# The embedding gate of a four-block kernel: both passes by rows, eight units each, with its first four weight units in homes of their own

## The reference

```python
gate, up = jnp.split(rms_norm_2(h, g_ffn_pre) @ w_ffn_in, 2, axis=-1)
h = h + rms_norm_2((jax.nn.silu(gate) * up) @ w_ffn_out, g_ffn_post)
e = p_i @ w_ple_proj
h = h + rms_norm_2(jax.nn.sigmoid(h @ w_ple_gate) * e, g_ple_post)
return h
```

## Time and profile before

| | us |
|---|---|
| median of three runs | 1835.9 |
| lowest and highest | 1835.85, 1836.21 |
| the profiled execution's own time | 1835.64 |
| its span, first to last instruction | 1833.8 |
| TensorE matmuls busy | 1816.5 |
| VectorE busy | 1197.2 |
| ScalarE busy | 983.3 |
| GpSimd busy | 127.9 |

### The profile page before, as it was taken

How to read it: one execution, slowest core, us unless ns; L and a number is a source line. 1 busy time by engine, 2 the same in 40 slices (tenths; PEclk the granted TensorE clock), 3 DMA queues, 4 the chain that set the end, 5 groups by cost and what they waited for, 6 DMA issues and landing times.

```text
span 1833.8 us, 24654 instructions
## 1 busy us (share of the span) xinstructions
PE 1816.5 (99%) x8930; PEld 1502.5 (82%) x8930; DVE 1197.2 (65%) x2064; ACT 983.3 (54%) x1565; POOL 127.9 (7%) x52
## 2 busy tenths in 40 slices
PE   8999999999999999999999999999999999999998
PEld 7887888888888888888877888888877788888886
DVE  6766873556776874455767867555677686675556
ACT  5556554444555654445655656544557366464444
POOL 0000018300000008500000000000000000000000
PEclk9999999999999999999999999999999999999999
DMA  7544555556544655555644445656556354555563
GB/s 248 154 140 136 195 193 175 184 191 194 169 144 138 198 167 188 180 186 178 197 144 142 147 161 172 206 158 211 173 169 194 104 167 139 175 178 187 174 211 109
DMA packets 167771, 315.31 MB, mean 172 GB/s; under 512 B 10250, under 2 KB 22748, under 8 KB 167524
## 3 DMA queue, kind: packets, MB, share of 16 engines
q1 hardware_dynamic: 167332, 313.14, 53.6%
q10 hardware_dynamic: 320, 0.60, 0.1%
HBM read 312.65 MB, written 1.05 MB: 171 GB/s over the span
## 4 chain that ended last, share of the span: by engine, by line
PE 95%; DVE 3%; issue 1%; ACT 1%; DMA 0%; ACTq 0%; DVEq 0%
PE acc L598 84%; PE mix L565 4%; PE mix L850 1%; PE mix L657 1%; PE mix L645 1%; PE mix L863 1%; DVE lo L1576 1%; PE mix L891 1%; PE mix L904 1%; PE mix L625 1%; PE mix L825 0%; PE mix L922 0%; PE mix L839 0%; PE mix L859 0%; PE mix L830 0%
## 5 line engine op out<-in xcount | busy, mean ns | idle before, releaser
L1109 ACT ACTIVATE hi<-raw 128x1024 fp32r<-128x1024 f32 (+3 forms) x596 | 612.0, 1032 | 518.5 <-PE acc L598 487.5
L1576 DVE TENSOR_TENSOR lo<-raw,hi 128x1024 fp32r<-128x1024 f32 (+3 forms) x548 | 641.7, 1186 | 232.5 <-ACT hi L1109 218.0
L598 PE MATMUL acc<-hi,xTh 128*128 128x512 f32 (+3 forms) x1712 | 669.5, 391 | 1.3 <-DVE xTl L1615 1.3
L598 PE MATMUL acc<-hi,xTl 128*128 128x512 f32 (+3 forms) x1712 | 653.9, 382 | 0.0
L598 PE MATMUL acc<-lo,xTh 128*128 128x512 f32 (+3 forms) x1712 | 652.9, 381 | 0.0
L598 PEld LDWEIGHTS acc<-hi,xTh 128*128 128x128 f32 x1712 | 322.4, 188 | 69.9 <-issue 9.4
L598 PEld LDWEIGHTS acc<-hi,xTl 128*128 128x128 f32 x1712 | 322.2, 188 | 62.3
L598 PEld LDWEIGHTS acc<-lo,xTh 128*128 128x128 f32 x1712 | 322.7, 188 | 57.8 <-issue 1.0
L1077 POOL TENSOR_TENSOR lo<-raw,hi 128x1024 fp32r<-128x1024 f32 x48 | 127.6, 2688 | 634.7 <-ACT hi L1109 634.7
L598 PE MATMUL acc<-hi,hTh 128*128 128x512 f32 x432 | 169.0, 391 | 0.0
L598 PE MATMUL acc<-hi,hTl 128*128 128x512 f32 x432 | 168.2, 389 | 0.0
(11 more groups left out here) (255 smaller groups left out, 1671.1 us busy)
## 6 DMA issues: line engine op xcount, KB each, us to landing
raw<-in_w_in SPq DMA_DIRECT2D x192, 512.0 KB, 3.5
raw<-in_w_ffn_in SPq DMA_DIRECT2D x80, 512.0 KB, 4.4
raw<-in_w_mlp_up SPq DMA_DIRECT2D x64, 512.0 KB, 3.6
raw<-in_w_mlp_down SPq DMA_DIRECT2D x64, 512.0 KB, 4.4
raw<-in_w_ffn_out SPq DMA_DIRECT2D x44, 512.0 KB, 4.5
raw<-in_w_out SPq DMA_DIRECT2D x32, 512.0 KB, 4.3
raw<-in_w_o_gla SPq DMA_DIRECT2D x16, 512.0 KB, 3.7
raw<-in_w_o_attn SPq DMA_DIRECT2D x16, 512.0 KB, 3.8
```

What stands on the lines that cost most here:

```text
L598: last = nc.tensor.matmul(out, a[:, t * P:(t + 1) * P], w[:, part, :], start=(k == 0 and a is ah and w is hi), stop=(k == c.k_tiles - 1 an ...
L1109: nc.scalar.activation(L.plan.part(L.hi, u, L.hi_early), L.plan.part(L.raw, u), ACT.Copy).then_inc(*n.up("hi_ready"))
L1576: v.tensor_tensor(lo, raw, hi.bitcast(F32), ALU.subtract).then_inc(*n.up("low_by_dve"))
```

## The change

The gate is done for row 0 in units 152 to 159, with the eight transposes of row 1 after unit 155, and then for row 1 with its halves turned round: 156 to 159 first, then 152 to 155 (`turn`). The transposes for the gate put four k tiles in a bank, and ScalarE and VectorE split a bank in one instruction of 128x512. Units 152 to 155 of blocks 2 and 3 have homes for highs and lows outside the ring: two in the arena of the attention part, two in the tiles over the hidden rows, where the last block's first two units also lie; its third and fourth go into the ring. In block 2 the transposes of block 3's row 0 stand between the two halves of row 1. The opening of block 3 does four units for row 0 (three before) ahead of row 1's transposes. The orders on ScalarE and VectorE are written anew. The number of signals for banks falls by two each on banks 0 and 2.

```diff
@@ Plan
-        self.early = {self.base[-1] + i: i for i in range(RING)}
+        gates = [self.base[ln] + PLE_FIRST for ln in range(LAYERS, BLOCKS)]
+        self.early = {u + i: (i // 2, i % 2) for u in gates for i in range(RING)}
+        self.early.update({self.base[-1] + i: (1, 2 + i) for i in range(2)})
...
+    def turn(self, u):
+
+        i = u - self.base[self.unit[u][0].ln] - PLE_FIRST
+        return u - i + (i + RING) % (2 * RING) if self.unit[u][0].name == "ple" else u
...
     def before(self, u):
-        return u - 2 * RING if u - RING in self.early else u - RING
+        v = u - RING
+        while v in self.early:
+            v -= RING
+        return v
@@ tensor_program
     def unit(u):
-        products(u, (1,) if u in begun else (0, 1), (1,) if u in halved else (0, 1)).then_inc(*n.up("unit_used"))
+        v = L.plan.turn(u)
+        products(v, (1,) if v in begun else (0, 1)).then_inc(*n.up("unit_used"))
...
-        turn_rows("g", 0, x_tile)
+        turn_rows("g", 0, x_tile, (0,))
         s.to(152)
-        rest_of_rows("g", 152)
-        s.to(156)
+        pe.wait_ge(*n.next("x_rows"))
+        turn_rows("g", 0, x_tile, (1,))
+        first_rows(156)
+        pe.wait_ge(*n.next("x_rows", NT))
+        turn_rows("g", 1, x_tile)
         first_rows(160)
         if ln + 1 < BLOCKS:
-            s.to(159)
-            products(s.plan.base[ln] + 159, (1,), (0,))
+            s.to(156)
             ln += 1
             pe.wait_ge(*n.next("x_rows"))
             turn_rows("x", 0, x_tile)
             ln -= 1
-            halved.add(s.u)
         s.to(160)
...
-        first_rows(u + (3 if tag == "x" else 2))
-        pe.wait_ge(*n.next("x_rows"))
+        first_rows(u + (4 if tag == "x" else 2))
+        pe.wait_ge(*n.next("x_rows", 2 if tag == "x" else 1))
         turn_rows(tag, 1, x_tile)
@@ scalar_program, opening of block 3
+            squares_of_row(0)
             s.to(1)
             split_rows("x", 1, x_gain(ln))
-            squares(L.x, 0)
             s.to(2)
             split_half("x", 1, x_gain(ln))
-            squares(L.x, 1)
+            squares_of_row(1)
@@ scalar_program, the gate
         square_of(b, 0)
         root(VAR_X, POST, 1)
-        s.to(151)
-        split_rows("g", 0)
+        s.to(150)
+        split_rows("g", 0, banks=(0,))
         square_of(b, 1)
         root(VAR_X + 1, POST + 1, 1)
         s.to(152)
         embedded(L.plan.chunk(ln, "plain", COLS))
-        s.to(153)
+        split_rows("g", 0, banks=(1,))
+        s.to(157)
         split_rows("g", 1)
-        s.to(154)
-        split_half("g", 1)
...
-        s.to(157)
...
         if ln + 1 < BLOCKS:
             highs(opening + 3)
-        gated(a, 1)
-        if ln + 1 < BLOCKS:
-            highs(opening + 4)
-        s.to(159)
-        if ln + 1 < BLOCKS:
             ln += 1
             split_rows("x", 0, x_gain(ln))
             ln -= 1
-            gated(b, 1)
-            s.to(160)
-            gated_square(a, 1)
-        else:
-            gated(b, 1)
-            gated_square(a, 1)
+            highs(opening + 4)
+        gated(a, 1)
+        gated_square(a, 1)
+        gated(b, 1)
         gated_square(b, 1)
@@ vector_program, opening of block 3
-            s.to(1)
+            s.to(2)
             gated_with_gain(a, 1)
             dve.wait_ge(*n.next("squared", 2))
             mean_of_rows(1)
             inverse_root_of_rows(1)
             add_normed(1, 0)
-            s.to(2)
-            split_rows("x", 1, x_gain(ln))
-            gated_with_gain(b, 0)
             gated_with_gain(b, 1)
             tell("gain2_free")
-            add_normed(0, 1)
+            split_rows("x", 1, x_gain(ln))
             add_normed(1, 1)
@@ vector_program, the gate
         refine(0)
         add_normed(0, 0)
+        s.to(150)
+        add_normed(0, 1)
         s.to(151)
-        split_rows("g", 0)
+        split_rows("g", 0, banks=(0,))
         dve.wait_ge(*n.next("squared"))
         mean_of_rows(1, "variance")
         s.to(152)
         refine(1)
         add_normed(1, 0)
-        s.to(154)
         with_gain(b, 1, 1)
         tell(f"pair{b.pair}_drained")
         tell("gain1_free")
+        add_normed(1, 1)
+        split_rows("g", 0, banks=(1,))
+        s.to(158)
         split_rows("g", 1)
-        add_normed(0, 1)
-        add_normed(1, 1)
-        s.to(155)
-        split_half("g", 1)
         gain_landed(2)
...
-        s.to(158)
         gated(a, 0)
-        gated_with_gain(a, 0)
-        if ln + 1 < BLOCKS:
-            opening = L.plan.base[ln] + L.plan.size[ln]
-            lows(opening + 1)
-            gated(b, 0)
-        else:
-            gated(b, 0)
-            gated_with_gain(b, 0)
+        if ln + 1 == BLOCKS:
+            gated_with_gain(a, 0)
+        gated(b, 0)
+        gated_with_gain(*((a if ln + 1 < BLOCKS else b), 0))
...
         if ln + 1 < BLOCKS:
+            opening = L.plan.base[ln] + L.plan.size[ln]
             add_normed(0, 0)
             lows(opening + 2)
-            s.to(160)
-            sigmoid_read(a)
             ln += 1
             split_rows("x", 0, x_gain(ln))
             ln -= 1
+            s.to(160)
+            sigmoid_read(a)
             gated(a, 1)
+            gated_with_gain(b, 0)
+            add_normed(0, 1)
             sigmoid_read(b)
             gated(b, 1)
         else:
+            add_row(0)
             gated(a, 1)
             tell(f"pair{a.pair}_drained")
-            add_row(0)
```

More of the change, by code:

```diff
@@ L109 @@
 RING = 4
+PLE_FIRST = 152
 I32 = mybir.dt.int32
@@ L285, in by_rows, with used, ends_of @@
     def by_rows(self, c, j):
[L287 removed]
+        return c.ln >= LAYERS and (c.tag == "g" or j < 2 and (c.tag == "f" or c.tag == "x" and c.ln > LAYERS))
+    def turn(self, u):
+        i = u - self.base[self.unit[u][0].ln] - PLE_FIRST
+        return u - i + (i + RING) % (2 * RING) if self.unit[u][0].name == "ple" else u
+    def used(self, u):
+        return self.turn(u) + 1
+    def ends_of(self, c, t):
+        return (self.turn(c.first), self.turn(c.final)) if c.name == "ple" and t else (c.first, c.final)
     def part(self, ring, u, early=None):
         c = self.unit[u][0]
[L292 removed]
+        home, slot = self.early[u] if early is not None and u in self.early else (None, u % RING)
+        tiles = ring if home is None else early[home]
         return tiles[:, slot, 0:min(2, c.k_tiles), 0:c.n]
     def before(self, u):
[L297 removed]
+        v = u - RING
+        while v in self.early:
+            v -= RING
+        return v
     def chunk(self, ln, name, to):
@@ L574, in tensor_program, with products @@
     y_tile = lambda t, k: L.y[:, t, k * P:(k + 1) * P]
-    def products(u, rows, tiles=(0, 1)):
+    def products(u, rows):
         c, j = L.plan.unit[u]
         hi, lo = L.plan.part(L.hi, u, L.hi_early), L.plan.part(L.lo, u, L.lo_early)
-        if u == c.first and c.turn:
+        first, final = L.plan.ends_of(c, rows[-1])
+        if u == first and c.turn:
             if c.after_rows and rows == (0,):
@@ L591, in products @@
         pe.wait_ge(*n.at(*L.plan.low[u]))
-        for part in tiles[:c.k_tiles]:
+        for part in range(min(2, c.k_tiles)):
             k = 2 * j + part
@@ L614, in first_rows, with turn_rows @@
                 last.then_inc(*n.up("rows0_done"))
-    def turn_rows(tag, t, rows):
-        for j in range(2):
-            fill((tag, "rows", t, j), lambda b: [nc.tensor.transpose(L.mix[:, b, i * P:(i + 1) * P], rows(t, 2 * j + i), L.ident) for i in range(2)])
+    def turn_rows(tag, t, rows, banks=(0, 1)):
+        tiles = 4 if tag == "g" else 2
+        for j in banks:
+            fill((tag, "rows", t, j), lambda b: [nc.tensor.transpose(L.mix[:, b, i * P:(i + 1) * P], rows(t, tiles * j + i), L.ident) for i in range(tiles)])
     def scores(tag, h, q, k):
@@ L1104, in high @@
         if u in L.plan.early:
-            out = next(c for c in L.plan.chunks if c.ln == BLOCKS - 2 and c.weight == "w_ffn_out_2" and c.to == COLS)
-            act.wait_ge(*n.at("unit_used", out.final + 1))
+            out = [c for c in L.plan.chunks if c.weight == "w_ffn_out_2" and c.to == COLS and c.first < u][-1]
+            if L.plan.early[u][0]:
+                act.wait_ge(*n.at("unit_used", out.final + 1))
         elif u >= RING:
-            act.wait_ge(*n.at("unit_used", L.plan.before(u) + 1))
+            act.wait_ge(*n.at("unit_used", L.plan.used(L.plan.before(u))))
         nc.scalar.activation(L.plan.part(L.hi, u, L.hi_early), L.plan.part(L.raw, u), ACT.Copy).then_inc(*n.up("hi_ready"))
@@ L1197, in squares, with squares_of_row @@
             square(rows[:, t, g * COLS:(g + 1) * COLS], parts + 2 * g + t)
+    def squares_of_row(t):
+        for g in range(2):
+            act.wait_ge(*n.next("x_rows"))
+            square(L.x[:, t, g * COLS:(g + 1) * COLS], PARTS + 2 * g + t)
     def softmax_exp(tag, h, scale):
@@ L1622, in split_half, with split_rows @@
             split(tag, j, gain=gain)
```

(4 more changed lines are left out.)

34 lines of the change are left out of this document (17 added, 17 removed).

## The result

| | before | after |
|---|---|---|
| median, us (five runs each) | 1835.85 | 1843.69 |
| lowest and highest | 1834.02, 1836.21 | 1843.56, 1844.73 |
| the profiled execution's own time | 1835.64 | 1843.56 |
| its span | 1833.8 | 1841.7 |

After over before is 1.0048, with an interval of 1.0037 to 1.0059: 7.8 us slower. The spans of the two profiled executions differ by 7.9 us, so the two traces can be laid side by side and have to account for all of it. The five times before and after don't overlap.

What follows compares the result with a forecast made beforehand. TensorE's matmul stream, busy 99% of the span, was taken as the bound. Two gates of 5.2 us (10.4), opening +0.5 and end -0.3 gave +10.6 on 1835.64: 1846.2 us, range 1840 to 1850.5.

Steps and rivals of the forecast that it cites:

- VectorE's order holds low 154: Gate, VectorE: four things newly ahead of low 154 make it ready at 1322.7, where TensorE comes to it at 1319.2.
- Low 153 stands for its high: Gate: ScalarE makes high 153 behind row 1's root, so VectorE stands 1.46 us before low 153.
- The split of 128x512: Gate, VectorE: each wide split out of PSUM takes 0.70 us, bounded by 0.69 and 0.76.
- The stall, 3.5 in each gate: TensorE waits 3.5 us for low 154 before unit 154 in blocks 2 and 3; bounds 2.0 to 3.7.
- The late load, +0.7: Gate: unit 158's load waits for low 154; TensorE waits 0.4 there, some 0.3 at 159; bounds 0 to 2.0.
- The clock, +1.7 in each gate: Behind each gate's stall TensorE's clock falls as in the old opening, costing 1.7 us and swallowing the late load's 0.7.
- The forecast's words for a clock that stays at 1.00: Sign: if row-0 products break in the gate but the clock stays at 1.00, the time is 1843 to 1844.
- The opening, +0.5: Block 3's opening: waits of 2.8 become 2.8 to 3.8 at other places, with the same clock fall; 0.5 us more.
- The end, -0.3: Program's end: row 0 ends earlier, so the gated product starts at about 1826.5 instead of 1826.80; 0.3 us gained.
- the smaller stall: Rival, 14%: high 153 doesn't hold VectorE, 2.0 us per gate, and no clock fall behind it; +4.3, 1840.
- The worse loads: Rival, 10%: loads take 5.6 us to land, unit 158 waits some 2 us in each gate; +14.1, 1850.
- The faster one: Rival, 6%: homes bring highs and lows ahead of need, block 3's opening loses its gaps and clock fall; -4.8, 1831.

Runs made afterwards that it cites:

- Experiments 1: Kernel after, with VectorE's lows 154 and 155 moved ahead of y, the second add of x and the second split: 1838.02 us, ratio 1.0014.
- experiment 5: Kernel before, with VectorE's y for row 1's second half and both second-half adds of x put ahead of lows 154 and 155: 1838.93 us, ratio 1.0019.
- experiment 2: Kernel after, with ScalarE's high 153 made ahead of row 1's square and root: 1840.87 us, ratio 1.0025.
- experiment 6: Kernel after, with SyncE holding the load of block 3's first unit until high 159 of block 2 is ready: 1844.14 us, ratio 1.0047.
- Experiment 9: Kernel of 7, with ScalarE's high 155 ahead of its second split and VectorE's two signals behind its split: 1834.56 us, ratio 0.9995.
- experiment 3: Kernel after, with lows 154 and 155 moved ahead on VectorE and high 153 moved ahead on ScalarE: 1836.27 us, ratio 1.0005.
- experiment 4: Kernel before, with homes outside the ring for highs and lows of units 152 and 153 in both gates: 1835.77 us, ratio 0.9999.
- 7: Kernel of experiment 3, with lows of the opening's units 2 and 3 ahead of VectorE's sigmoid read: 1835.38 us, ratio 0.9999.
- 10: Kernel of Experiment 9, with three units instead of four for row 0 ahead of row 1's transposes in block 3's opening: 1834.65 us, ratio 0.9995.
- experiment 8: Kernel of 7, with low 156 of both gates made by GpSimd instead of VectorE: 1835.37 us, ratio 0.9999.

## Why the prediction was right

The forecast was 1846.2, in a range of 1840 to 1850.5, with 0.89 on slower; 1843.69 came out, slower by 0.43%. The way and the mechanism are right; the size is 2.5 us too large, and the term that was mis-sized most is the clock. By its own steps:

- **VectorE's order holds low 154.** Right, and the main step. Low 154 started at 1321.04 where 1321.35 was worked out. From the add of x(0, first half) to it the forecast had 11.3 us, the trace 10.8 (1310.23 to 1321.04). Experiments 1 and 5 show it from both sides: taken out of after, the wait shrinks from 2.76 to 0.44; put into before, one of 1.53 appears.
- **Low 153 stands for its high.** Right: 1.32 us for 1.46, and experiment 2 gave 1.3 back in each gate.
- **The split of 128x512.** It lasts 0.68, but the next instruction starts 0.60 behind it (1314.08 to 1314.68), and the forecast's chain adds such distances. So its 0.70 was 0.1 too much, twice, and its lower bound of 0.69 too high.
- **The stall, 3.5 in each gate.** The mechanism is right and the size 0.6 too large: 2.9, twice. The chain was 0.5 us shorter than forecast: 0.2 by the two splits, 0.1 by the stand for high 153, and the rest by the lows, which follow at 1.14 and not 1.18. TensorE came to unit 154 0.1 later (behind the transposes ahead of unit 152 the second product starts 0.32 us after the first, 1316.94 after 1316.62, and not 0.23).
- **The late load, +0.7.** Mis-sized, inside its bounds of 0 to 2.0, and it fell on another unit. Unit 158 was to be late by 0.4 and 159 by 0.3. The load of 158 landed in 3.6 us and wasn't late; that of 159 took 5.9, with two more issued behind it within some 2.3 us, and was late by 1.6 in block 2. In block 3, where no loads follow, it took 4.5. That is most of why there is no wait there: low 159 is done at 1820.01, 7.9 us behind the start of unit 154, and TensorE at full clock would want it after 7.8. The fall of the clock swallowed only the 0.2 that would have been left with the hand-over. The fit that the forecast took from the Trainium skill, "DMA: Bandwidth & Descriptors", section "Anatomy of one DMA — SWDGE (gpsimd) path", is for loads issued by GpSimd; its estimate of 3.2 us for 512 KB lies under all of these loads, which SyncE issued. The nearest to it is the 3.6 us of a load that started with no other in flight.
- **The clock, +1.7 in each gate.** This is the term that carries most of the error. The forecast took one fall before as a rule for every gap of its size and expected three. The profiled execution after had one, behind a wait of 2.77 us, and none behind the same wait 490 us earlier. Net of the opening, where the fall of before stayed away, the clock cost 0 where +3.4 was forecast. The forecast's words for a clock that stays at 1.00, 1843 to 1844, fit the number but not the trace: there was a fall in block 3, and one less in the opening. That they fit is partly luck. The three falls that were forecast did come in experiment 6, with the same waits at unit 154, and that execution took 1845.15.
- **The opening, +0.5.** Right that waits are exchanged: 3.1 us, at the places named, for a forecast of 2.8 to 3.8. Before has 3.0 when it is read by starts, so the difference is +0.1. "The same fall" was wrong, -1.7.
- **The end, -0.3.** Right: -0.25.

The forecast with the measured terms in place of its own: 3.4 less for the clock, 1.2 less for the two stalls, 1.6 more for the load (its sum held nothing for it, since the fall was to swallow it), 0.4 less in the opening's waits. 1846.2 - 3.4 - 1.2 + 1.6 - 0.4 = 1842.8, and the profiled execution took 1843.56. Of the 0.8 between them, 0.2 is the beginning and 0.2 the slow second products behind the new holes, neither of them in the forecast; 0.4 is rounding or isn't assigned. That the stall was too large (1.2) and the load too small (1.6) cancelled is luck. The weak step is the one from a single fall in the trace of before to a rule for every gap of its size.

Of the rivals, the smaller stall (1840) had one reason wrong, as high 153 did hold VectorE, and one half right: there was one example of a fall, and behind one of the two gaps none came. The worse loads (1850) had the right mechanism for block 2, but on unit 159 and not 158, 1.6 us for some 2, and once and not twice. The faster one, 1831, needed low 154 done by 1319.2. Experiment 9 shows that this can be had by order alone, and that the gain is then still not 4.8: waits of 0.4 and 1.2 us stay in the opening, and one of 0.4 in block 2's gate.

## What to carry to other kernels

Where orders are written out by hand, list for each engine what the new order puts ahead of the next thing that the busiest engine needs, and sum it against the slack; here the place of two lines cost 7.4 of the 7.8 us, the homes were free, the turned halves were worth 4 us once the orders were right, and with both lines in place the whole change lay within 0.4 us of before. A buffer that is free early helps only if the producers' orders reach the unit early, and each late low passes its delay on through the slot that it frees to the load four units on. Before a change is given up, look for the one or two lines of order that hold it: the same design with four lines of order added and two signals moved (experiment 9) lies 9 us lower.

## What the runs showed of the hardware that was not expected

**The clock doesn't fall behind every gap of one size.** In the profiled execution after, two waits of 2.76 and 2.77 us with the same instructions around them were followed by a clock of 1.00 and by 0.80, 0.50, 0.50, 0.50. In experiment 6 both such waits were followed by 0.50. The opening shows the same with smaller waits: behind 0.91 and 1.19 us, with four transposes between, the clock fell in the traces of experiments 1, 2 and 6 and not in those of after and experiment 3; behind 1.14 and 0.69 it fell in before and experiment 5 and not in experiment 4. Single waits of up to 1.53 us (experiments 2, 5, 7 to 10) had no fall behind them in any trace. The times of the kernel before agree with that: over its 84 runs in three batches those with a mean clock of 0.999 have a median of 1834.5 us, the others, two in three, 1836.2. A mean clock doesn't say where it fell, but the difference of 1.7 us is the 1.7 read from the earlier trace rows, so a fall there that comes and goes from run to run is the likely reason. What decides it is open. In experiments 9 and 10, where no wait but those at the program's start is longer than 1.5 us, all 22 runs are at 0.999.

**Loads close together.** In block 2's gate after, 512 KB landed in 3.6 us for the first of four loads, and in 5.9, 6.0 and 6.1 us for the three issued behind it, each some 1.1 us after the one before.

**VectorE beside GpSimd.** In experiment 8 an add of 128x512 took 1.98 us in place of 0.75 while GpSimd made a low of 128x1024 (2.47 us), and the same again in block 3.
